# Routing each tile in the recurrence, and scattering its rows to per-expert regions in DRAM

## What is computed

```
t  = h.reshape(B * L, D)
lg = t @ w_router_group + b                      # 4 groups
gi = argmax(lg)
le = (t @ w_router_expert + b)[group gi]         # 4 experts of that group
top_v, top_i = top_k(softmax(le), 2)
wts = softmax(lg)[gi] * top_v / sum(top_v)
for e in range(16):
    hid = silu(t @ w_gate[e]) * (t @ w_up[e])    # 1024 -> 512
    out += comb[:, e:e+1] * (hid @ w_down[e])    # 512 -> 1024
```

## Time and profile before

| | us |
|---|---|
| median of 3 runs | 1582.14 |
| lowest, highest | 1575.85, 1586.65 |
| profiled execution | 1577.13 |
| its span, first to last instruction | 1575.4 |

### The profile page before, as it was taken

How to read it: one execution, slowest core, us unless ns; L and a number is a source line. 1 busy time by engine, 2 the same in 40 slices (tenths; PEclk the granted TensorE clock), 3 DMA queues, 4 the chain that set the end, 5 groups by cost and what they waited for, 6 DMA issues and landing times. The chain is left out here.

```text
span 1575.4 us, 28583 instructions
## 1 busy us (share of the span) xinstructions
PE 1446.2 (92%) x12005; PEld 1042.5 (66%) x12005; DVE 526.7 (33%) x988; ACT 371.3 (24%) x766; POOL 184.1 (12%) x303
## 2 busy tenths in 40 slices
PE   5799999999996899999999999964999999999965
PEld 3466666566664877777777777634887878788831
DVE  4244644530211454544544544346000010000017
ACT  5231331311212323224223223120101111111122
POOL 1002112110001212102102102001000000000043
PEclk9899999999998999999999999985999999999988
DMA  8337566441233621321321311026969997888457
GB/s 319 112 98 238 175 201 227 161 145 60 78 102 134 220 58 52 109 52 59 108 60 51 108 36 41 1 60 226 341 229 378 380 392 295 311 327 327 158 206 262
DMA packets 167856, 271.70 MB, mean 172 GB/s; under 512 B 18336, under 2 KB 88862, under 8 KB 167728
## 3 DMA queue, kind: packets, MB, share of 16 engines
q1 hardware_dynamic: 153504, 222.47, 42.0%
q0 software_dynamic: 11920, 38.99, 6.5%
q10 hardware_dynamic: 2304, 8.39, 1.3%
HBM read 215.22 MB, written 54.59 MB: 171 GB/s over the span
## 5 line engine op out<-in xcount | busy, mean ns | idle before, releaser
L2162 PEld LDWEIGHTS banks<-moe_xT,moe_wg 128*128 128x128 f32 x1024 | 131.3, 191 | 8.9 <-issue 7.8
L2162 PE MATMUL banks<-moe_xT,moe_wg 128*128 128x128 f32 (+4 forms) x1024 | 135.3, 290 | 0.8 <-ACT moe_xT L2265 0.8
L2162 PE MATMUL banks<-moe_xT,moe_wu 128*128 128x128 f32 (+4 forms) x1024 | 134.5, 290 | 0.9 <-DMA moe_wu<-w_expert_up 0.9
L2162 PEld LDWEIGHTS banks<-moe_xT,moe_wu 128*128 128x128 f32 x1024 | 131.2, 191 | 1.1 <-DMA moe_wu<-w_expert_up 1.1
L1548 POOL TENSOR_TENSOR mixer_LTm<-mixer_LT,level 128x256 f32<-128x256 f32 (+1 forms) x90 | 72.0, 822 | 401.7 <-ACT mixer_LTo L1605 276.2
L653 PE MATMUL banks<-xT,w_v 128*128 128x352 f32 (+1 forms) x384 | 118.7, 469 | 0.0
L653 PE MATMUL banks<-xT,w_r 128*128 128x352 f32 (+1 forms) x384 | 118.6, 469 | 0.0
L653 PE MATMUL banks<-xT,w_k 128*128 128x352 f32 (+1 forms) x384 | 118.3, 468 | 0.0
L1275 PE MATMUL banks<-mixer_w_out,mixer_yT 128*128 128x512 f32 x256 | 115.3, 607 | 0.0
L2191 PE MATMUL banks<-moe_wd,moe_hid 128*128 128x512 f32 x256 | 112.5, 592 | 0.0
L653 PEld LDWEIGHTS banks<-xT,w_v 128*128 128x128 f32 x384 | 72.6, 190 | 45.2 <-issue 2.2
(11 more groups left out here) (457 smaller groups left out, 1944.3 us busy)
## 6 DMA issues: line engine op xcount, KB each, us to landing
moe_wg<-w_expert_gate SPq DMA_DIRECT2D x16, 2048.0 KB, 9.4
moe_wu<-w_expert_up SPq DMA_DIRECT2D x16, 2048.0 KB
moe_wd<-w_expert_down SPq DMA_DIRECT2D x16, 2048.0 KB, 11.3
feats<-w_ada SPq DMA_DIRECT2D x8, 2048.0 KB
wada<-w_ada SPq DMA_DIRECT2D x4, 2048.0 KB
feats<-w_ada_final SPq DMA_DIRECT2D x4, 2048.0 KB
expert_rows<-moe_yrow ACTq DMA_DIRECT2D x16, 512.0 KB, 6.2
expert_rows<-moe_xTo SPq DMA_DIRECT2D x16, 512.0 KB
```

The costliest lines, as they stand in the source:

```text
L2162: mm = pe.matmul(bank[:, i * n:(i + 1) * n], wt[:, p % 2, q, (t0 + i) * P:(t0 + i + 1) * P], xT[:, p % 2, q, 0:n], start=q == 0, stop=q == ...
```

## The change

Three parts.

1. **Routing in the recurrence.** At the end of front(n) VectorE routes tile n-1 alone (`route`, 15 instructions), since its logits are there. In the next front TensorE computes the ranks of that tile (`rank(n-2)`, two small matmuls ahead of level 3: one over the tile's own choices, one over the sum of all earlier tiles), VectorE turns rank and choice into a row number (`route_rows`: region of the expert, `CAP` = 1152 rows apart, plus rank), and GpSimd scatters the tile's 128 rows of h2 to these rows of a new DRAM tensor `xs`, once for each of the two choices. The store of h2 stays for tiles 7 and 8 alone. `norm` waits for the scatters in place of the store.
2. **Zero rows.** In the projection GpSimd writes zeros to the first 192 rows of each region, behind features(0) for eight experts and behind features(1) for the others. After the last expert's load it zeroes 64 rows behind each expert's last row.
3. **Experts.** Tiles 7 and 8 are ranked and scattered at the block's start (tile 8 is routed there too). The order of experts follows. The one-hot matrices, the plan and the gathers go. `take` loads plain slices of `xs`: 128 rows for a main tile, one slice for each expert in a tail tile; the row is read from `order` by a register. Slots (still needed by the combine), shares and blocks are computed after the first tiles are turned, and behind experts 0 and 1.

The core of the diff:

```diff
+def route_rows(V, then, c, n, made):
+    then(V.tensor_tensor(c["slot16"][:, :], c["rank"][:, n, :], c["first_row"][:, :], ALU.add))
+    then(V.tensor_tensor(c["slot32"][:, :, :], c["slot16"][:, :].unsqueeze(1).to_broadcast([P, 2, NE]), c["chosen"][:, n, :, :], ALU.mult))
+    then(V.tensor_reduce(out=c["row_f"][:, :], in_=c["slot32"][:, :, :], axis=AX_X, op=ALU.add))
+    V.tensor_copy(c["row"][:, n, :], c["row_f"][:, :]).then_inc(made, 1)
...
 # projection, GpSimd
+            def static_rows(experts):
+                pool.wait_ge(sg("zeros_made"), 1)
+                for e in experts:
+                    for lo, hi in ((0, P), (P, S_MAX)):
+                        pool.dma_start(d["xs"][e * CAP + lo:e * CAP + hi, :], zeros[0:hi - lo, :]).then_inc(sg("xs_zeroed"), 16)
             for j in range(NJ):
                 features(j)
+                if j < 2:
+                    static_rows(range(8 * j, 8 * j + 8))
...
 # recurrence, TensorE: ahead of level 3
+            def rank(i):
+                w(pe, "either_made", i + 1)
+                w(pe, "taken_added", i)
+                w(pe, "TI0_made", 6 * (i + 2) + 3)
+                mm = pe.matmul(psum[2][:, 256:256 + NE], c["after"][:, :], c["either"][:, i, :], start=True, stop=i == 0)
+                if i:
+                    mm = pe.matmul(psum[2][:, 256:256 + NE], ones[:, :], c["taken_so_far"][:, :], start=False, stop=True)
+                mm.then_inc(sg("ranked"), 1)
...
 # recurrence, GpSimd: end of front(n)
+                if n >= 2:
+                    pool.wait_ge(sg("rows_found"), n - 1)
+                    pool.wait_ge(sg("h2_made"), n - 1)
+                    for i in range(2):
+                        pool.indirect_dma_start(out=d["xs"], out_offset=bass.IndirectOffsetOnAxis(ap=c["row"][:, n - 2, i:i + 1], axis=0),
+                                                in_=h2[:, :], in_offset=None).then_inc(sg("h2_scattered"), 16)
...
 # recurrence, VectorE: norm, update(3), ahead of update(4), end of front
-                    w(dve, "h2_stored", 16 * (n - 1) + 1)
+                    if n <= NP:
+                        w(dve, "h2_scattered", 32 * (n - 1))
...
+                    if k == 3 and n >= 2:
+                        ranks(n - 2)
...
+                if n >= 2:
+                    rows_of(n - 2)
                 update(4)
...
+                if not first and m_next:
+                    dve.wait_ge(sg("rt_read"), n)
+                    route(V, then, c, n - 1, sg("either_made"))
...
 # experts, GpSimd
+            for u, m in ((0, P), (1, DEC)):
+                pool.wait_ge(sg(f"h2_loaded{u}"), 16)
+                pool.wait_ge(sg("rows_found"), u + 1)
+                for i in range(2):
+                    pool.indirect_dma_start(out=d["xs"], out_offset=bass.IndirectOffsetOnAxis(ap=c["row"][0:m, NP - 1 + u, i:i + 1], axis=0),
+                                            in_=xg[0:m, u, :], in_offset=None).then_inc(sg("h2_scattered"), 16)
+            pool.wait_ge(sg("order_made"), 1)
+            pool.wait_ge(sg("lanes_made"), 1)
+            pool.wait_ge(sg("h2_scattered"), 64)
             def take(i):
                 kind, at = TILES[i]
                 w(pool, "turned1", i - 1)
-                pool.indirect_dma_start(out=xg[:, i % 2, :], out_offset=None, in_=d["h2"],
-                                        in_offset=bass.IndirectOffsetOnAxis(ap=plan_token[:, col:col + 1], axis=0)).then_inc(sg(f"x{i % 2}_loaded"), 16)
+                if kind == "main":
+                    pool.dma_start(xg[:, i % 2, :], d["xs"][bass.ds(first_row(at), P), :]).then_inc(sg(f"x{i % 2}_loaded"), 16)
+                    return
+                for p in range(NE):
+                    n, lane = tail_of(p), TAIL_AT[p] - at * P
+                    if n and 0 <= lane < P:
+                        pool.dma_start(xg[lane:lane + n, i % 2, :], d["xs"][bass.ds(first_row(p) + S_MAIN, n), :]).then_inc(sg(f"x{i % 2}_loaded"), 16)
...
 # experts, VectorE
+            tail_rows(0)
+            route(V, then, c, NP, sg("either_made"))
+            tail_rows(1)
             dve.wait_ge(sg("counted"), 1)
...
-            dve.wait_ge(sg("plan_done"), 1)
-            V.tensor_copy(plan_token[:, :], psum[2][:, 0:NTILE]).then_inc(sg("plan_made"), 1)
...
+            sizes()
             put_tail(0)
             put_main(0)
+            rows()
             for p in range(NE):
                 expert(p)
+                if p == 0:
+                    shares()
+                if p == 1:
+                    blocks()
```

More of the change, by code:

```diff
@@ L119, in build @@
             "by_place": sb("by_place", [P, 2, NE]),
+            "earlier": sb("earlier", [P, 4, 4]),
+            "first_row": sb("first_row", [P, NE]),
+            "group": sb("group", [P, NT, NG]),
+            "le": sb("le", [P, NT, EG]),
+            "place4": sb("place4", [P, NT, EG]),
+            "either": sb("either", [P, NT, NE]),
+            "chosen": sb("chosen", [P, NT, 2, NE]),
+            "rank": sb("rank", [P, NT, NE]),
+            "taken_so_far": sb("taken_so_far", [P, NE]),
+            "route": [sb(n, [P, 4, 4]) for n in ("ahead", "beats", "tmp16")],
+            "four": [sb(n, [P, 4]) for n in ("place_g", "top2", "picked")],
+            "slot16": sb("slot16", [P, NE]),
+            "slot32": sb("slot32", [P, 2, NE]),
+            "row_f": sb("row_f", [P, 2]),
+            "row": sb("row", [P, NT, 2], I32),
         }
@@ L137, in bank4, with route, places, grouped @@
     return bank[:, :].rearrange("p (a b) -> p a b", a=4)
+def route(V, then, c, n, made):
+    ahead, beats, tmp16 = c["route"]
+    place_g, top2, picked = c["four"]
+    logits, group, le, place4 = [c[name][:, n, :] for name in ("logits", "group", "le", "place4")]
+    def places(v, out):
+        then(V.tensor_tensor(ahead[:, :, :], v.unsqueeze(1).to_broadcast([P, 4, 4]), v.unsqueeze(2).to_broadcast([P, 4, 4]), ALU.subtract))
+        then(V.tensor_tensor(beats[:, :, :], ahead[:, :, :], c["earlier"][:, :, :], ALU.is_gt))
+        then(V.tensor_reduce(out=out, in_=beats[:, :, :], axis=AX_X, op=ALU.add))
+    def grouped(v):
+        return v.rearrange("p (g e) -> p g e", g=NG)
+    by_group = group.unsqueeze(2).to_broadcast([P, NG, EG])
+    def by_member(v):
+        return v[:, :].unsqueeze(1).to_broadcast([P, NG, EG])
+    places(logits[:, 0:NG], place_g[:, :])
+    then(V.tensor_scalar(group, place_g[:, :], 0.0, None, ALU.is_equal))
+    if n == NP:
+        then(V.memset(c["group"][DEC:P, n, :], 0.0))
+    then(V.tensor_tensor(tmp16[:, :, :], grouped(logits[:, NG:]), by_group, ALU.mult))
+    then(V.tensor_reduce(out=le, in_=tmp16[:, :, :].rearrange("p g e -> p e g"), axis=AX_X, op=ALU.add))
+    places(le, place4)
+    then(V.tensor_scalar(top2[:, :], place4, 1.5, None, ALU.is_lt))
+    V.tensor_tensor(grouped(c["either"][:, n, :]), by_group, by_member(top2), ALU.mult).then_inc(made, 1)
+    for i in range(2):
+        then(V.tensor_scalar(picked[:, :], place4, float(i), None, ALU.is_equal))
+        then(V.tensor_tensor(grouped(c["chosen"][:, n, i, :]), by_group, by_member(picked), ALU.mult))
+def route_rows(V, then, c, n, made):
[3 more added lines that the diff above has]
+    V.tensor_copy(c["row"][:, n, :], c["row_f"][:, :]).then_inc(made, 1)
 def over4(mask):
@@ L1703, in _, with then @@
             V = nc.vector
+            routed = [0]
+            def then(op):
+                routed[0] += 1
+                op.then_inc(sg("route_step"), 1)
+                dve.wait_ge(sg("route_step"), routed[0])
             dve.sem_inc(sg("x1_stored"), 1)
@@ L1979, in experts_block, with loads_of, loaded @@
             TILES.append(("main", p_))
+        def loads_of(i):
+            kind, at = TILES[i]
+            return 1 if kind == "main" else len([p_ for p_ in range(NE) if tail_of(p_) and TAIL_AT[p_] // P == at])
+        def loaded(i):
+            return 16 * sum(loads_of(j) for j in range(i % 2, i + 1, 2))
         def tail_tile(g):
@@ new lines, in rows @@
+            def rows():
+                then(V.tensor_tensor(slot[:, :, :], rank[:, :, :], each(main_at), ALU.add))
+                then(V.scalar_tensor_tensor(past1[:, :, :], rank[:, :, :], float(S_MAIN), each(tail_by), ALU.is_ge, ALU.mult))
+                then(V.tensor_tensor(past2[:, :, :], rank[:, :, :], each(taken_place[:, 0, :]), ALU.is_ge))
+                then(V.tensor_tensor(past2[:, :, :], past2[:, :, :], each(over_by), ALU.mult))
+                for past in (past1, past2):
+                    then(V.tensor_tensor(slot[:, :, :], slot[:, :, :], past[:, :, :], ALU.add))
+                then(V.tensor_tensor(taken[:, :, :, :], slot[:, :, :].unsqueeze(2).to_broadcast([P, NT, 2, NE]), chosen[:, :, :, :], ALU.mult))
+                then(reduce(slot_f[:, :, :], taken[:, :, :, :], ALU.add))
+                then(V.tensor_copy(slots[:, :, :], slot_f[:, :, :]))
@@ new lines, in shares @@
+            def shares():
+                for i in range(2):
```

(16 more changed lines are left out.)

266 lines of the change are left out of this document (120 added, 146 removed).

## The result

| | before | changed |
|---|---|---|
| median, us | 1578.99 (4 runs) | 1609.58 (4 runs) |
| lowest, highest | 1574.51, 1586.65 | 1604.01, 1612.94 |
| ratio, 95% interval | | 1.0187 (1.0155 to 1.0218) |
| profiled execution; span | 1577.1; 1575.4 | 1612.9; 1611.5 |

The change makes the kernel 30 us slower, where 6 us faster was forecast. To see where they went, I cut both spans at the same five events of TensorE's timeline: the first product of the recurrence, the first and the seventh router product, the end of the ninth, and the first gate product. Three later versions (experiments 1, 6 and 13) are cut the same way.

The account below looks back on a forecast made before the run. TensorE bounds recurrence and expert stage; the 40.4 us hole between them can be won back. Hole -11.4, clock +0.5, recurrence +3.5, projection +1 sum to -6.4 us: 1570.7 profiled, 1575.7 median, range 1566 to 1589.

Parts of the forecast that it names:

- the price of the zeros in the projection: Projection: two batches of zero writes delay the modulation weights by 0 to 6 us in all; 1 us taken.
- the third rival: Projection: zeros served ahead of modulation weights, TensorE waits 3 us in each of two pieces; 1580.7 us, chance 0.12.
- my two cases: Projection: weights get half the rate and land at 157; or zeros all go first and weights land at 162 to 165.
- The hole: TensorE's 40.4 us between last router product and first gate product: new chain of ranks, scatters and loads gains 11.4 us.
- the 0.5 us for a later rise of the clock: First gate product: clock may rise later, up to 2 us at 1.2 GHz, losing 1 us; 0.5 taken.
- The first rival, fast loads: Hole: the experts' row loads land in 3 us, gain 15.7; 1571.4 us, chance 0.15.
- The recurrence: Recurrence: rank products 3.1 us plus 0.4 in half tile 8, VectorE's other work hidden; cost 3.5 us.
- The rank products: Recurrence: 13 small matmuls on TensorE, with no idle time to hide them, cost 3.1 us in full.
- Moved by 1.05 and run back to back they end at about 874.7: nothing: Recurrence: row-number instructions ahead of update 4 delay its four instructions by 1.05 us, covered by VectorE's idle 0.79; no cost.
- In the half tile 8 these covers are shorter: 0.4 us: Recurrence, half tile 8: less VectorE idle time covers the added instructions, costing 0.4 us.
- the second rival: Recurrence: VectorE's 15 routing instructions overrun each tile's end; at 0.6 us each 18 us lost, 1594 us, chance 0.08.
- The expert stage: Expert stage: plain loads replace gathers, added computations and zeroing are hidden, weight traffic is the same; no cost.

Follow-up runs that it names:

- experiment 1: The changed kernel with the same zero writes issued late, in the projection's second part, four experts behind each of four stores: 1581.9 us, ratio 1.002.
- experiment 6: The changed kernel with late zeros, row numbers found behind update 5, and rank products ahead of the second set of scores: 1572.0 us, ratio 0.9959.
- 13: The changed kernel with zeros, rows and rank products all moved later, timed again on another chip: 1565.4 us, ratio 0.993.
- experiment 2: The kernel before with only the zero writes added, in their first place, into a tensor nothing reads: 1615.3 us, ratio 1.0236.
- experiment 3: The changed kernel with zeros in half-size batches, four experts behind each of pieces 0 to 3: 1589.2 us, ratio 1.0068.
- 7: The changed kernel with late zeros, rows and ranks, first up and down weights held until two tiles of rows landed: 1576.0 us, ratio 0.9995.
- 15: The kernel before with only the zero writes added, in the late place: 1576.9 us, ratio 1.0003.
- experiment 10: The changed kernel with late zeros, rows and ranks, all first expert weights held until two tiles of rows landed: 1579.4 us, one run.
- 5: The changed kernel with late zeros, and a tile's row-number instructions moved from ahead of update 4 to behind update 5: 1573.4 us, ratio 0.9967.
- experiment 11: The changed kernel with late zeros, rows and ranks, VectorE doing the routing of each full tile twice: 1581.0 us, one run.
- the three moves: Zeros, row-number instructions and rank products all moved later in the changed kernel, timed on two chips: 1572.0 and 1565.4 us, ratios 0.9959 and 0.993.
- 4: The changed kernel, zeros in their first place, each write described as two halves of 512 columns a row: 1613.7 us, ratio 1.0215.

## Why the prediction was wrong

**The step that failed is the price of the zeros in the projection** ("So 0 to 3 us a batch, 0 to 6 us in all. I take 1, because only the worst order of service reaches the limit"). It was 29 us in the changed kernel and 35 in experiment 2. The mechanism had been named, as the third rival, with 3 us in each of two pieces; the rival's size was off by a factor of five. Four things were left out; in the changed kernel the second, the rate, weighs most:

- The time at half clock behind a wait. The sum priced a stall at its length. The two waits make 25.8 us; 29.1 were lost, and in experiment 2 35.0 for waits of 25.5.
- The rate. The bound took 399 GB/s from a window of weight loads. This stretch moved 245 to 361 GB/s with all engines busy; experiment 3 gives 270 for the zeros on top of the other traffic. At that price 6.3 MB take 23 us and not 15.8, 7 us more for each batch.
- The queue ahead. GpSimd had issued four feature stores of 544 KB from 136.1 to 139.7, just ahead of the zeros. Of their 2.2 MB, 1.2 MB were still to be moved at 140, and the first packet of zeros starts at 143.0, 2.8 us after its issue.
- The order of service. Neither of my two cases (half and half, zeros all first) was right: nothing until 150, then a third. The rule that I weighed fits: the Trainium skill, page DMA: Bandwidth & Descriptors, section Queues, rings and completion order, has an engine go round its queues packet by packet. The counts 317 to 312 and 323 to 328 agree, if the trace's packets are the page's. With a third of 350 GB/s from 151 on, 2.1 MB would be there at 169. In the trace nine tenths of the weights' packets have started by 167.2, but the last one starts at 171.7, and TensorE also waits for the bias loads queued behind, until 174.4.

That this rule "gives the second case", the zeros first, was a wrong reading of it. It cost little: in the trace the last zeros land at 173.5 and the last of the weights and biases at 174.4, so these end with the whole volume.

**The hole** was right. Forecast 11.4 less 0.5, measured 10.2. The last load is issued 18.9 us after the last router product, against 18.1. The first turn, the tail tile's, follows 6.5 later; the main tile's load landed 8.5 us after its issue by its semaphore (7.3 taken, with 1 for the tail tile; median landing of all such loads 7.1). The scatters took 4.2 us from the last issue to the load (3.0 taken), and the first gate group took 5.44 us as before, so the 0.5 us for a later rise of the clock were not lost here. In 1, 6, 7 and 13 this group took 7.0 to 7.9 us, but also in 2 and 15, which have the old chain, so that isn't shown to be the change's. The first rival, fast loads, was decided by experiment 10: a landing of 3.4 to 4.0 us exists, but only without the gate's 2 MB.

**The recurrence** was mis-sized: 3.5 us forecast, 17.3 measured. By its parts:

- The rank products cost 0.35 us a tile (58.97 in 5 against 58.62 before), some 2.2 in all (3.1 taken), and 0.09 a tile where TensorE waits anyway (experiment 6).
- "Moved by 1.05 and run back to back they end at about 874.7: nothing" was wrong by 0.34 us a tile (59.31 in 1 against 58.97 in 5). The idle 0.79 us ahead of the scores' mask does cover the mask, which starts 3.13 us after the start of the mask before it in both kernels. But update 4 itself is late: its last instruction starts 2.73 us after the start of that mask where it was 2.06, and the next level's product waits for it. TensorE's row in a tile of the changed kernel, which in the kernel before has no idle time:

```profile
677.94 0.59 PE L1326 MATMUL banks<-mixer_XX,mixer_TT 64*64 64x64 f32 x7 [0.31 <-issue]
```

- "In the half tile 8 these covers are shorter: 0.4 us": TensorE waited 1.16 us, then ran at 0.57 of its clock for 12. The last stretch lost 4.2 us; with the rows moved it is 94.3 to 97.4, as in the kernels without the change.
- The first stretch, +7.5 in the profiled execution, is not shown to be the change's. It has a spell at half clock behind a wait of 1.43 us with no releaser in the view. With the change it lies between 100.8 us (experiment 3) and 108.8, without it between 101.3 (before) and 108.8 (experiment 15, which has the same wait of 1.43 us).
- One more of the six tiles than before is a disturbed one, 1.5 us longer, as some are in every kernel.

**VectorE's routing at a tile's end** (the second rival) shows no cost in the profile; within the tiles even twice of it did not (experiment 11). **The expert stage** was as forecast: 476.8 against 477.0.

With the three moves the kernel is 0.4 to 0.7% faster than before, 7 and 11 us, so the forecast of -6.4 describes a version with these costs taken out. That it comes so near is in part luck, since the same kernel gave both numbers. For the change as it stood, the range (1566 to 1589) was built from a bound that was none.

## What to carry to other kernels

A batch of writes that nobody waits for is paid by whoever shares the DMA engines: add up all bytes queued in all queues ahead of and beside the next load that has a deadline, divide by the rate of that very stretch, and price a stall with the time at low clock behind it. Put such a batch where the DMA share is low and no load has a near deadline; here that alone was worth 26 to 28 us in the changed kernel and 37 in the kernel before (ratios 1.0236 and 1.0003). And small instructions on a helper engine are free only where nothing that another engine waits for stands behind them: of two places 6.6 us apart in its program one cost 0.34 us a tile, the other at most 0.09.

## What the runs showed of the hardware

- Two queues with work had equal numbers of packets served (312 and 317, 328 and 323 in 5 us), and a load issued while the other queue was full had one packet in its first 5 us (428 in the kernel before, in the same window).
- The zeros went in packets of 4096 bytes whether a row was written as a whole, as two pieces or as half rows; another DMA added 16 packets of 4 bytes.
- The same 16 engines, all busy, moved 399 GB/s of weight loads, and 245 to 361 GB/s of zero writes, the first almost alone and the others beside loads.
- An idle 0.96 us of TensorE was followed by 10 us at about 1.2 GHz (PEclk 0.54 and 0.50); an idle 1.68 us in experiment 1 by none (the product after it took 1.96 us, as at full clock). Ahead of that same product an idle 2.17 us in 13 was followed by 0.61 of the clock for 4 us, an idle 2.67 us in 4 by full clock. Single tiles were 1.5 us longer in all kernels, also in the one before (60.16 and 60.19 against 58.62); in the changed kernel such a tile lies over a window at 0.66 of the clock from 765 to 770. What decides it, the runs don't show.
- A load of 512 KB landed 4.0 us after its issue with no weights in flight (10), 8.8 with 2 MB of weights (7) and 8.5 with 6 MB (6).
